# Constant products in four waits of TensorE, the last down unit in two parts, and the rows of x turned ahead of the gains

## The reference, cut to what matters

```python
h = concatenate([meta, x])                        # 16 + 256 = 272 rows of 1024
# layer 0
p = rms_norm(h, e_norm) @ e_w_in
y = concatenate([rwkv7_mix(p[..., :1792], ...), rglru_mix(p[..., 1792:2304], p[..., 2304:], ...)])
h = h + y @ e_w_out
h = h + hier_moe(rms_norm(h, m_norm[0]), ...)
# layer 1
h = h + gla_mix(rms_norm(h, o_norm) @ o_w_in, ...) @ o_w_out
h = h + hier_moe(rms_norm(h, m_norm[1]), ...)
out = rms_norm(h[:, 16:], final_norm)

def hier_moe(...):       # 32 experts, each row goes to the best two of one group of eight
    for e in range(32):
        hid = silu(hf @ w_gate[e]) * (hf @ w_up[e])
        y = y + (hid @ w_down[e]) * combine[:, e:e + 1]
```

## Time and profile before

| | |
|---|---|
| timed, median of 3 | 971.07 us (971.05 to 971.64) |
| profiled execution | 976.18 us, its span 974.7 us |
| TensorE busy | 793.2 us (81%), weight loads 542.4 us |
| VectorE busy | 371.3 us (38%) |
| ScalarE busy | 180.0 us (18%) |
| mean granted TensorE clock | 0.919 of full speed |
| loaded and stored | 242.03 MB |

### The profile page before, as it was taken

The page is one execution under the profiler, slowest core; times in us unless marked ns, Lnnn a source line. Parts: engine busy times, 40 slices in busy tenths (PEclk is TensorE's granted clock), DMA queues, the critical chain, the costliest instruction groups (busy, mean ns, idle before and its releaser), DMA issues.

```text
span 974.7 us, 16703 instructions
## 1 busy us (share of the span) xinstructions
PE 793.2 (81%) x7482; PEld 542.4 (56%) x7482; DVE 371.3 (38%) x736; ACT 180.0 (18%) x349; POOL 10.4 (1%) x50
## 2 busy tenths in 40 slices
PE   6999667984968988889987999998496987668764
PEld 5877557871566554645543878876155543434431
DVE  3537757636134333143324135533515222022112
ACT  3153322230040000000002152402013000000002
POOL 4000000000000000000000000000000000000000
PEclk9999968997969999899998999997797998898887
DMA  9545210003446999989999441003354999999993
GB/s 276 152 138 179 108 66 3 3 3 143 203 172 257 420 420 421 421 347 422 420 420 370 142 130 61 27 19 156 133 230 160 421 420 421 419 422 421 421 421 146
DMA packets 61091, 242.03 MB, mean 248 GB/s; under 512 B 9414, under 2 KB 33084, under 8 KB 36060
## 3 DMA queue, kind: packets, MB, share of 16 engines
q1 hardware_dynamic: 60956, 240.94, 62.6%
q10 hardware_dynamic: 64, 0.02, 0.0%
HBM read 239.90 MB, written 1.05 MB: 247 GB/s over the span
## 4 chain that ended last, share of the span: by engine, by line
PE 62%; DMA 22%; DVE 10%; issue 2%; ACT 2%; SPq 1%; ACTq 0%; DVEq 0%; PEldq 0%
PE ps L1133 11%; DMA M<-in_m_w_down_dram 10%; PE ps L988 8%; PE ps L723 8%; PE ps L885 6%; DMA M<-in_m_w_gate_dram 6%; DMA M<-in_m_w_up_dram 6%; PE ps L953 5%; PE ps L1024 4%; PE ps L966 3%; PE ps L840 2%; PE ps L825 2%; PE ps L808 1%; PE ps L731 1%; PE ps L1112 1%
## 5 line engine op out<-in xcount | busy, mean ns | idle before, releaser
L988 PE MATMUL ps<-M 128*32 128x256 f32 x2048 | 129.7, 410 | 43.7 <-DMA M<-in_m_w_gate_dram 33.4
L988 PEld LDWEIGHTS ps<-M 128*32 128x32 f32 x2048 | 74.0, 118 | 109.0 <-issue 65.8
L1133 PE MATMUL ps<-M 128*128 128x272 f32 (+3 forms) x464 | 107.0, 389 | 1.0 <-DVE M L1234 1.0
L1133 PEld LDWEIGHTS ps<-M 128*128 128x128 f32 (+2 forms) x464 | 82.1, 179 | 22.8 <-issue 3.1
L953 PE MATMUL ps<-M 128*128 128x128 f32 x688 | 86.6, 289 | 6.7 <-DVE M L1621 4.0
L953 PEld LDWEIGHTS ps<-M 128*128 128x128 f32 x688 | 84.3, 204 | 7.8 <-DVE M L1621 4.9
L723 PE MATMUL ps<-M 128*128 128x272 f32 x352 | 84.6, 403 | 0.9 <-DVE M L1234 0.9
L1553 DVE TENSOR_TENSOR H<-H,ps 128x512 f32<-128x512 f32 x68 | 46.8, 688 | 89.9 <-PE ps L966 89.6
L1024 PE MATMUL ps<-M 128*32 128x512 f32 x512 | 62.2, 629 | 20.3 <-DMA M<-in_m_w_down_dram 15.6
L723 PEld LDWEIGHTS ps<-M 128*128 128x128 f32 x352 | 68.6, 196 | 16.1 <-issue 1.4
L966 PE MATMUL ps<-M 128*128 128x512 f32 x136 | 68.3, 624 | 10.0 <-DVE H L1556 6.8
(11 more groups left out here) (319 smaller groups left out, 868.6 us busy)
## 6 DMA issues: line engine op xcount, KB each, us to landing
M<-in_m_w_gate_dram SPq DMA_DIRECT2D x32, 2048.0 KB, 18.7
M<-in_m_w_up_dram SPq DMA_DIRECT2D x32, 2048.0 KB, 24.6
M<-in_m_w_down_dram SPq DMA_DIRECT2D x32, 2048.0 KB, 25.5
M<-in_o_w_in_dram SPq DMA_DIRECT2D x12, 1024.0 KB, 5.5
M<-in_e_w_in_dram SPq DMA_DIRECT2D x11, 1024.0 KB, 5.9
M<-in_e_w_out_dram SPq DMA_DIRECT2D x1, 4096.0 KB, 15.8
M<-in_o_w_out_dram SPq DMA_DIRECT2D x1, 4096.0 KB, 16.2
H<-in_x_dram SPq DMA_DIRECT2D x2, 512.0 KB, 4.5
```

The lines of the kernel that those rows point to most:

```text
L988: ins = pe.matmul(ps[32 * e:32 * e + 32, 3 * x, 0:FF], xgT[q % 2][:, k, 32 * e:32 * e + 32], gu_w[UNIT_SLOT[u]][:, e, k, :], start=(k == 0 ...
L1133: ins = pe.matmul(ps[rows, unit % 4, 0:n], lhs(k), rhs(k), start=(k == 0), stop=(k == KD - 1))
```

## The change

Five edits:

- `keep_busy(n, bank)` makes n products of the all-ones matrix with itself, 128x512, into a PSUM bank whose contents nobody reads any more. It is called four ways: two products at TensorE's start; four in `out_proj` once two of the four mixed parts are there; four behind the last logits; two behind the ranks.
- `mix_ready` becomes `mix_part`, raised behind each of the four parts; TensorE's fillers wait for the second, all else for the fourth.
- The blocks of x and the meta rows are turned first, and the gains behind them into bank 4; VectorE's copy of the gains moves behind the three diagonals.
- The last down unit's two transfers get a semaphore each (`ld_last0`, `ld_last1`). TensorE makes the products of its first two experts when the first has landed, those of the other two when the second has.
- The number of units in a slot is counted without that last unit.

```diff
-UNITS_A_SLOT = NU // 4
+UNITS_A_SLOT = [UNIT_SLOT[:NU - 1].count(j) for j in range(4)]
...
                     elif u == 1:
-                        sp.wait_ge(s("mix_ready"), y + 1)
+                        sp.wait_ge(s("mix_part"), 4 * y + 4)
...
                     for h in range(2):
+                        landed = s(f"ld_last{h}") if u == NU - 1 else s(f"ld_s{j}")
                         sp.dma_start(slots[j][:, 2 * h:2 * h + 2, :], src[:, 4 * q + 2 * h:4 * q + 2 * h + 2, :]) \
-                            .then_inc(s(f"ld_s{j}"), 16)
+                            .then_inc(landed, 16)
...
             pe.wait_ge(s("consts"), 1)
-            pe.wait_ge(s("ld_gn"), 64)
-            pe.transpose(ps[:, 7, 288:320], gnr, ident[0:32, 0:32]).then_inc(s("gn_tr"), 1)
+            def keep_busy(n, bank):
+                for _ in range(n):
+                    pe.matmul(ps[:, bank, :].rearrange("p (a c) -> p a c", a=4), ones[:, :],
+                              ones[:, :].unsqueeze(1).to_broadcast([P, 4, P]), start=True, stop=True)
+
+            keep_busy(2, 7)
...
             for n in range(3):
                 pe.wait_ge(s(f"ld_x{n}"), 16)
-                if n == 0:
-                    turned(n, range(7))
-                    pe.wait_ge(s("gn_set"), 1)
-                    turned(n, range(7, KD))
-                else:
-                    turned(n, range(KD))
+                turned(n, range(KD))
+            pe.wait_ge(s("ld_gn"), 64)
+            pe.transpose(ps[:, 4, 288:320], gnr, ident[0:32, 0:32]).then_inc(s("gn_tr"), 1)
             spread(0, (0, 1, 2))
...
             def out_proj(y):
                 pe.wait_ge(s("ld_wout"), 16 * (y + 1))
-                pe.wait_ge(s("mix_ready"), y + 1)
+                pe.wait_ge(s("mix_part"), 4 * y + 2)
+                keep_busy(4, 5)
+                pe.wait_ge(s("mix_part"), 4 * y + 4)
...
                 logits(1).then_inc(s("lg_done"), 1)
+                keep_busy(4, 6)
...
                 ins.then_inc(s("rk_done"), 1)
+                keep_busy(2, 6)
...
-                    loaded(u)
-                    for hf in range(2):
-                        for k in range(2):
-                            for e in range(4):
-                                r = slice(32 * e, 32 * e + 32)
-                                ins = pe.matmul(ps[r, 4 + hf, :], hidT[:, k, r], dn_w[UNIT_SLOT[u]][:, e, k, 512 * hf:512 * hf + 512],
-                                                start=(k == 0), stop=(k == 1))
-                        ins.then_inc(s("dn_done"), 1)
+                    if q < NQ - 1:
+                        loaded(u)
+                    for es in (range(0, 2), range(2, 4)) if q == NQ - 1 else (range(4),):
+                        if q == NQ - 1:
+                            pe.wait_ge(s(f"ld_last{es[0] // 2}"), 16 * (y + 1))
+                        for hf in range(2):
+                            for k in range(2):
+                                for e in es:
+                                    r = slice(32 * e, 32 * e + 32)
+                                    ins = pe.matmul(ps[r, 4 + hf, :], hidT[:, k, r],
+                                                    dn_w[UNIT_SLOT[u]][:, e, k, 512 * hf:512 * hf + 512], start=(k == 0), stop=(k == 1))
+                            if es[-1] == 3:
+                                ins.then_inc(s("dn_done"), 1)
```

More of the change, by code:

```diff
@@ L982, in loaded @@
                 def loaded(u):
-                    pe.wait_ge(s(f"ld_s{UNIT_SLOT[u]}"), 32 * (UNITS_A_SLOT * y + UNIT_TURN[u] + 1))
+                    pe.wait_ge(s(f"ld_s{UNIT_SLOT[u]}"), 32 * (UNITS_A_SLOT[UNIT_SLOT[u]] * y + UNIT_TURN[u] + 1))
                 def half_gu(u, q, x):
@@ L1231, in entry @@
                         .then_inc(s("diag"), 1)
+                if y == 0:
+                    v.wait_ge(s("gn_tr"), 1)
+                    v.tensor_copy(gnT[:, :, :].rearrange("p n k -> p (n k)"), ps[:, 4, 288:320]).then_inc(s("gn_set"), 1)
+                    v.wait_ge(s("gn_set"), 1)
                 v.wait_ge(s("rb_set"), 3 * y + 3)
@@ L1235, in entry @@
                         .then_inc(s("xn"), 1)
-            v.wait_ge(s("gn_tr"), 1)
-            v.tensor_copy(gnT[:, :, :].rearrange("p n k -> p (n k)"),
-                          ps[:, 7, 288:320]).then_inc(s("gn_set"), 1)
             v.wait_ge(s("consts"), 1)
@@ L1430, in _ @@
                 link(tt(oT[:, j, PAD:TP], oT[:, j, PAD:TP], BV[:, j, PAD:TP], ALU.add))
-                ins = tt(mixT[:, j], oT[:, j, PAD:TP], GT[:, j, PAD:TP], ALU.mult)
-            ins.then_inc(s("mix_ready"), 1)
+                tt(mixT[:, j], oT[:, j, PAD:TP], GT[:, j, PAD:TP], ALU.mult).then_inc(s("mix_part"), 1)
             def experts(y):
@@ L1724, in _ @@
                     ins = tt(mixT[:, 2 * h + x], oG[:, 2 * h + x, PAD:TP], rr[:, 2 * h + x], ALU.mult)
-            ins.then_inc(s("mix_ready"), 1)
+                ins.then_inc(s("mix_part"), 1)
             experts(1)
```

## The result

The changed kernel takes 947.21 us (median of 4 runs, 945.75 to 948.65), the kernel before 971.36 beside it (4 runs, 971.05 to 975.83). The ratio is 0.9741, with a 95% interval of 0.9708 to 0.9774: by the medians a gain of 24.2 us, 22.0 to 28.4 by the interval.

The account below looks back on a forecast made before the run. Weight streams at 420 GB/s set the pace in two stretches; elsewhere TensorE pays for a low clock. Terms 2.5 + 2.0 + 2.15 + 4.2 + 1.85 + 2.35 + 1.65 = 16.7 us off the 971.07 median give 954.4 us, range 949.5 to 962.5.

Parts of the forecast that it names:

- the term of 2.5: Start: two fillers and the new turning order gain 2.5 us, between ends of 1 and 7.
- near the low end: Start: 2.5 us taken from ends 1 and 7, because 7 us of turning and waiting separate fillers from projections.
- rival 2: Start: the clock stays high through turning and projections, 7 us instead of 2.5, total 949.9 us; chance 13 in 100.
- the 1.5 that I put on the rule: Start: if transposes don't count as busy for the clock, the start gives only 1.5 us.
- a term of 0: States of layer 1: no edit there, no change of time in the sum.
- Output projections: Fillers in the wait for mixed parts cost nothing; gains of 2.0 us in the first layer, 2.15 in the second.
- Ranks and gathers: Fillers behind logits and ranks speed ranks and first gather: 4.2 us in the first layer, 1.85 in the second.
- The last down unit: Split in two parts, the second runs at the high clock behind the last transfer: gains of 2.35 and 1.65 us.
- filling the wait: Last down unit: the split hides nothing by itself; its first part, 3.5 to 3.67 us, fills the wait.
- 1, the split doesn't pay: Last down unit: column groups go one after another or the clock falls, losses 0.9 and 1.6, 960.9 us; chance 15 in 100.
- 3, constants don't raise the clock: All fillers: they cost only their delays, 977.4 us, or 973.4 with the down unit's gains kept; chance 6 in 100.
- 4, the streams swallow it: Whole kernel: the stream of weights sets the end and swallows the gain, 971 us; chance 5 in 100.

Follow-up runs that it names:

- e1: The kernel before with only the changed start (two fillers, x turned first, gains behind): 967.73 us, ratio 0.9956.
- e2: The changed kernel without the two fillers at the start, new order kept: 950.24 us, ratio 0.9778.
- e8: The kernel before once more, unchanged, for a second trace: 972.0 us, ratio 0.9992.
- e3: The changed kernel with the last down unit whole again, all products waiting for both halves, no fillers there: 950.95 us, ratio 0.9761.
- e12: The changed kernel with five more fillers ahead of the mixing's coupling products and four ahead of the overflow loop: 943.29 us, ratio 0.9701.
- e7: The changed kernel without any filler product, new start order and split kept: 970.75 us, ratio 0.9973.
- e14: The kernel before with 84 raises of an unused semaphore ahead of the second delta_in wait, where they are hidden: 965.18 us, ratio 0.9928.
- e9: The kernel before with 48 raises of an unused semaphore ahead of the first delta_in wait, not hidden: 974.77 us, ratio 1.0021.
- e10: The kernel before with 256 raises of an unused semaphore ahead of the first delta_in wait, not hidden: 1009.9 us, ratio 1.0382.
- e11: The changed kernel with 208 raises of an unused semaphore ahead of the first delta_in wait: 984.17 us, ratio 1.0121.
- e13: The kernel before with 48 raises of an unused semaphore ahead of the second delta_in wait, where they are hidden: 969.38 us, ratio 0.9975.
- e4: The changed kernel with the last down unit whole again and four fillers ahead of its wait: 947.26 us, ratio 0.9745.

## Why the prediction was right, and where it was wrong

**The start: the term of 2.5 was mis-sized; it measured 5.3** (5.0 in e1) against the second trace of the kernel before. Against the first, whose rows the term was priced on, it is 8.3, since that execution's own start was 2.9 us slower. The step that failed is "near the low end, since what stands between fillers and projections is 7 us of turning and waiting". Behind 3.69 us of fillers the turning runs at the high clock from its first record (1.84 and 1.69 us) and so is 3.5 us long, not 7; after it, about 1 us of small products and a wait of 1.0 us the projection takes 7.57, nearly the high clock's 7.35. That was rival 2, at 7. It had the mechanism of this trace, and 1.7 us too much for it. The forecast's own evidence, slow projections behind 6.8 us of turning, is of turning that begins low, as in e2 and e8; I carried it over to turning that begins high. It was not baseless: in e3 and e12 the clock does fall behind the fast turning, and the same landmark comes at 20.43 and 20.17 instead of 18.43, a start worth 3.3 to 3.6 us. Which of the two the timed executions mostly show isn't known; e1's 4.3 us lie between. By the Trainium skill (TensorE: Matmul & The Clock Gate, Part 4: PE-mode transpose) turning doesn't count as work for the clock. The traces agree with that only in part. A clock that was high through the turning is lost in e3 and e12 and kept in six others, and even in those two the start is worth 3.3 us and more, not the 1.5 that I put on the rule. And turning alone did raise the clock, which by the rule it should not; the row is the second half of the turning in e7, which has no fillers:

```profile
7.87 1.86 PE L696 MATMUL ps<-ident,H 128*128 128x16 f32 x16
```

The same took 3.43 us at the low clock in the first trace of the kernel before. In e7 the clock was lost again by the time of the projection (10.57 us), and so in e2 (2.23, then 9.25) and e8 (2.33, then 9.26).

**The states of layer 1: a term of 0 that measured 5.8.** The other step that failed is that the sum, without a reason given, let a stage with no edit keep its time. What the runs showed is a stop of TensorE for its own instructions. The instruction queue moved 60 blocks of 16384 bytes before as after, for some 15,200 records of products and weight loads of TensorE, so about one for 253 records. Ahead of the stop in the kernel before, one begins at 638.86 and the next not until 661.99, 542 records later, though the 256th record in between began at 658.4. The gate unit's two 2 MB transfers were issued at 654.94. The window of 0.8 us inside the stop, 661.8 to 662.6, by queue:

```profile
q1 hardware_dynamic: 47, 0.30, 90.0%
q8 instruction: 1, 0.02, 7.4%
```

The late block moves among 47 packets of weights, and TensorE goes on 1.5 us after it has landed. In the changed kernel the same block begins at 641.88, 1.3 us behind its 256th record instead of 3.6 (these times are the starts of single transfer and instruction records, counted from the span's start). With 84 raises it comes at 647.41, ahead of that kernel's gate unit (issued at 650.71), and nothing stops. In all the traces with a stop the block begins 4.4 to 7.3 us behind the issue of the gate unit, in the two without (e12, e14) 3.3 ahead of it. The delay alone is no sign of a stop: the next block of the kernel with 84 raises begins at 658.76, 3.3 us behind its 256th record and within the weights' transfer, and nothing stops; nor does it at 297.96 in the kernel before, as late, among long products. In the states ahead of the stop TensorE runs short ones: 157 product records and as many weight loads in 2.95 us, over a block's worth. Shown: that the place in the stream decides (e9, e10, e11, e13, e14), and that this one block falls into the transfer of weights wherever there is a stop. Only argued: that the weights' packets are what holds it up, and that short products are what makes it felt; a kernel with the gate unit issued later wasn't run.

The Trainium skill (Runtime: NRT & Kernel Launch, Instruction fetch mechanics) has instructions brought in blocks of 16 KiB or 256 instructions, at a cost that is "mostly hidden". The trace agrees on block and period, with 16384 bytes and e10's 256; here the cost wasn't hidden: 3.27 us, and some 2.7 more in the 20 slow records behind it.

**Output projections: right.** 5.54 to 3.65 and 22.96 to 20.87, so 1.9 and 2.1 us for 2.0 and 2.15.

**Ranks and gathers: right in sum, 6.1 us for 6.05, and wrong by layer.** Layer 0 gave 3.1 of 4.2: its fillers take 5.53 us as reckoned, but the logits ahead of them now run slow (3.27 us, at 0.50 in the window behind them), and the stretch up to the ranks is 1.2 us longer. Layer 1 gave 3.0 (5.1 less the 2.1 of the output projection) instead of 1.85, since there the logits ran at the high clock, 1.95 us instead of 2.88, which the sum had at 0. That these shifts cancel is luck; in e4, the same code up to there, the logits of layer 0 run high and that stretch is 1.4 us shorter than in the changed kernel.

**The last down unit: right in size (2.4 and 1.65), by a reason half as good.** Two column groups do go side by side: 16 records take 3.65. But what I called filling the wait is all there is to it, as e4 shows with constants in the place of the first half. Behind it layer 1's projection loses 1.6 us of clock (34.84 instead of 33.28; in e3 and e4 33.29), which wasn't in the sum and leaves 0.8 of the 2.4.

**The rivals.** 1, the split doesn't pay: out, by 3.65 us a part, though by what it costs behind it, it pays less than forecast. 3, constants don't raise the clock: out, by the windows above. 4, the streams swallow it: out, they are no longer than before and start earlier. A gain at a place that no edit touches was no case among them, and the range had no room for it.

**The base.** 954.4 stands on the median of 971.07, which was nearly right: 971.36 with the fourth run, and 971.6 to 973.4 in the later comparisons.

## What to carry to other kernels

A wait in which TensorE's clock falls can be filled with products of constants, and a chain of a few microseconds at the high clock is then worth about half of what it took at the low one; price each place by its own rows, and ask whether the clock that is raised lasts through the next small works too, in more than one trace, since executions of one kernel differ in it. Inserting or removing instructions shifts the boundaries of instruction blocks in everything behind, so that a stage nobody touched can change by 5 us: look for "issue" idle amid equal records, and before a gain is put down to an edit, run the kernel with as many empty instructions, placed where they are hidden. Effects of layout don't add: removing edits one at a time showed 15 us, removing all 23, and the traces put 5.6 of the difference into the states of layer 1, which none of them touches.

## What the runs showed of the hardware that was not expected

- TensorE can stop 3.0 to 3.5 us with nothing to wait for amid a burst of short products, with its next block of instructions arriving only inside the stop; 48 instructions more ahead make it 1.3 to 1.7, 84 none, and 256 bring it back.
- A raise of a semaphore on TensorE left 0.07 to 0.14 us of idle time where nothing hid it (3.17 us for 48, 35.18 for 256).
- Products of an all-ones matrix raise the granted clock as data does: 0.50 in their first 4.6 us, 0.99 in the window behind.
- The clock, raised by two fillers, outlasted 3.5 us of turning, 1 us of small products and 1 us of waiting in six traces and fell in two (7.57 or 9.26 us for the same 32 records); without fillers the same records took 9.25 to 10.57 us in every trace.
- Executions of the kernel before lie up to 8.3 us apart (970.5 to 978.8); its two traces differ in the start (23.76 or 26.70) and the coupling (22.33 or 24.01).
